# A two-layer sparse-attention encoder: an earlier first block of the gated units, and the copies of transposed probabilities moved from ScalarE to VectorE

## What is computed

```python
proj = h @ w_in                       # q, k, v, index q, index k, index weights, u
score = sum_h relu(iq_h @ ik) * iw_h  # keys are ranked by it, the best are kept
logits = q @ k / 8, others masked;  p = softmax(logits);  attn = p @ v
a, b = split(u);  g = a * sigmoid(b)  # gated units, 512 channels
y = silu(layer_norm(depthwise_conv31(g) + conv_b))
x = x + gate_a * (concat(attn, y) @ w_out)
x = x + gate_f * mixture_of_16_experts(norm(x))
```

## Time and profile before

| | us |
|---|---|
| median of 3 executions | 1450.54 (1449.70 to 1452.48) |
| the profiled execution's own time | 1449.31 |
| its span, first to last instruction | 1447.5 |
| TensorE / VectorE / ScalarE busy | 1253.6 / 569.4 / 368.4 |
| mean granted TensorE clock | 0.914 of full speed |

### The profile page before, as it was taken

The page is one execution under the profiler, slowest core; times in us unless marked ns, Lnnn a source line. Parts: engine busy times, 40 slices in busy tenths (PEclk is TensorE's granted clock), DMA queues, the critical chain, the costliest instruction groups (busy, mean ns, idle before and its releaser), DMA issues.

```text
span 1447.5 us, 16324 instructions
## 1 busy us (share of the span) xinstructions
PE 1253.6 (87%) x6291; PEld 733.4 (51%) x6291; DVE 569.4 (39%) x1478; ACT 368.4 (25%) x861; POOL 152.4 (11%) x218
## 2 busy tenths in 40 slices
PE   4898699987889998999837989899686999999990
PEld 0452254543545586777523533454345457777760
DVE  1227689123236531111107257980323455111115
ACT  2214120035741111111114133001468111111111
POOL 0312050010000150000020113200100011000002
PEclk7899899997999999999967989899858999999995
DMA  9428997260960479999953120224121016799985
GB/s 362 133 69 324 352 341 228 82 228 5 313 230 30 160 211 386 356 369 365 325 184 115 59 71 30 65 67 137 35 56 25 0 68 221 252 365 361 369 289 210
DMA packets 136887, 283.95 MB, mean 196 GB/s; under 512 B 11581, under 2 KB 91877, under 8 KB 130409
## 3 DMA queue, kind: packets, MB, share of 16 engines
q1 hardware_dynamic: 116128, 208.66, 42.7%
q0 software_dynamic: 8352, 42.50, 8.5%
q10 hardware_dynamic: 12329, 31.74, 6.2%
HBM read 236.86 MB, written 52.40 MB: 200 GB/s over the span
## 4 chain that ended last, share of the span: by engine, by line
PE 69%; DVE 11%; DMA 7%; ACT 6%; issue 3%; SPq 2%; ACTq 1%; POOLq 0%; POOL 0%; DVEq 0%
PE ps L508 44%; PE ps L813 9%; PE ps L518 5%; PE ps L671 3%; DMA W<-in_w_gate 3%; PE ps L732 3%; ACT arena L1194 2%; SPq L419 2%; DMA X<-in_x_sample 2%; DVE arena L1498 2%; PE ps L859 2%; DVE small L1497 1%; DVE arena L1537 1%; DVE arena L1588 1%; PE ps L632 1%
## 5 line engine op out<-in xcount | busy, mean ns | idle before, releaser
L508 PE MATMUL ps<-W,arena 128*128 128x256 f32 (+1 forms) x1280 | 348.1, 428 | 10.3 <-DMA W<-in_w_up 5.2
L508 PEld LDWEIGHTS ps<-W,arena 128*128 128x128 f32 x1280 | 242.2, 193 | 85.4 <-issue 49.9
L508 PE MATMUL ps<-W,hT 128*128 128x512 f32 (+3 forms) x480 | 195.0, 563 | 9.7 <-DVE gt L1369 6.6
L518 PE MATMUL ps<-C,arena 128*128 128x128 f32 (+3 forms) x835 | 118.4, 282 | 55.6 <-DVE arena L1417 18.1
L813 PE MATMUL ps<-W,hT 128*128 128x512 f32 (+1 forms) x320 | 144.7, 606 | 5.7 <-ACT hT L1251 5.7
L518 PEld LDWEIGHTS ps<-C,arena 128*128 128x128 f32 (+3 forms) x835 | 95.6, 148 | 96.6 <-issue 36.1
L508 PEld LDWEIGHTS ps<-W,hT 128*128 128x128 f32 (+1 forms) x480 | 87.4, 186 | 110.3 <-issue 83.4
L508 PE MATMUL ps<-hT,W 128*128 128x128 f32 (+1 forms) x512 | 129.4, 414 | 7.1 <-ACT arena L1118 7.1
L508 PEld LDWEIGHTS ps<-hT,W 128*128 128x128 f32 x512 | 79.1, 193 | 58.4 <-issue 50.5
L1805 DVE TENSOR_TENSOR arena<-arena,ps 128x256 f32<-128x256 f32 x32 | 13.5, 421 | 221.7 <-ACT arena L1292 221.7
L813 PEld LDWEIGHTS ps<-W,hT 128*128 128x128 f32 (+1 forms) x320 | 57.1, 183 | 79.9 <-issue 73.6
(11 more groups left out here) (250 smaller groups left out, 1174.1 us busy)
## 6 DMA issues: line engine op xcount, KB each, us to landing
W<-in_w_ada SPq DMA_DIRECT2D x48, 1024.0 KB, 7.4
W<-in_w_gate SPq DMA_DIRECT2D x32, 1024.0 KB, 10.6
W<-in_w_up SPq DMA_DIRECT2D x32, 1024.0 KB, 13.1
W<-in_w_down SPq DMA_DIRECT2D x32, 1024.0 KB, 7.8
y_d<-arena ACTq DMA_DIRECT2D x33, 512.0 KB, 7.3
W<-in_w_in SPq DMA_DIRECT2D x16, 1024.0 KB, 8.5
arena<-x_d SPq DMA_DIRECT2D x31, 512.0 KB, 11.5
arena<-arena SPq DMA_DIRECT2D x128, 79.2 KB, 2.1
```

What stands on the lines that cost most here:

```text
L508: ins = T.matmul(out, l, r, start=n == 0, stop=n == len(pairs) - 1, skip_group_check=True)
L518: count(T.transpose(o, i, ident[0:m, 0:m]), done if n == len(outs_ins) - 1 else None)
```

## The change

Two parts. TensorE's `u_block(0)` no longer waits for all 32 relus at its start: it waits for 30 of them before its first product into `ps[7]`. `u_block(1)` waits for 32 as before. And the copies of the transposed chunks are VectorE's (`copied`, a new function), first in each of its rounds; ScalarE's round becomes `normalised(n + 1)`, `outputs(n - 1)`, `exps(n + 2)`.

```diff
                 def u_block(i):

                     c = 3 + i // 2
-                    pe.wait_ge(*((s_glu, 4 * l + i - 1) if i >= 2 else (L["rel"], 32)))
+                    if i >= 2:
+                        pe.wait_ge(s_glu, 4 * l + i - 1)
+                    if i == 1:
+                        pe.wait_ge(L["rel"], 32)
                     for ab, smp in ((0, 0), (1, 0), (0, 1), (1, 1)):
+                        if i == 0 and smp and ab == 0:
+                            pe.wait_ge(L["rel"], 30)
...
-                for n, (t, g) in enumerate(GROUPS):
-                    m = rows_of(t)
+                for n in range(len(GROUPS)):
+                    if n + 1 < len(GROUPS):
+                        normalised(n + 1)
                     if n >= 1:
                         outputs(n - 1)
-                    for q, (c, kn) in enumerate(chunks_of(t)):
-                        job = PT0[n] + q
-                        act.wait_ge(L["pt"], job + 1)
-                        S.copy(pT[0:kn, c, 0:4 * m], ps[4 + job % 2][0:kn, 0:4 * m]).then_inc(L["pta"], 1)
-                    if n + 1 < len(GROUPS):
-                        normalised(n + 1)
                     if n + 2 < len(GROUPS):
                         exps(n + 2)
...
+                def copied(n):
+
+                    t, g = GROUPS[n]
+                    m = rows_of(t)
+                    for q, (c, kn) in enumerate(chunks_of(t)):
+                        job = PT0[n] + q
+                        dve.wait_ge(L["pt"], job + 1)
+                        V.tensor_copy(pT[0:kn, c, 0:4 * m], ps[4 + job % 2][0:kn, 0:4 * m]).then_inc(L["pta"], 1)
...
                 for n in range(len(GROUPS)):
+                    copied(n)
                     if n + 1 < len(GROUPS):
                         inverses(n + 1)
                     if n + 2 < len(GROUPS):
```

## The result

Forecast 1449.4 us, range 1445.0 to 1455.0. Measured: **1442.63 us**, median of 6 executions (1438.03 to 1446.21), against 1450.13 for the kernel before, 6 executions (1449.64 to 1456.18). The ratio is 0.9939, with a 95% interval of 0.9916 to 0.9963: 5 to 12 us faster, outside the range. The profiled execution took 1442.1 us, its span 1440.2 us (before 1447.5), its mean granted clock 0.916 (0.914).

A forecast was written before the change was run, and what follows sets the result against it. TensorE was taken as the bound, busy 1253.6 of 1447.5 us and 69% of the chain. Terms +2.4 - 11.7 + 7.0 + 1.2 = -1.1 us took the median 1450.5 to 1449.4 us, range 1445.0 to 1455.0.

The forecast's parts named there:

- Both first steps: Layer 1: the 7.13 us idle before `u_block(0)` return as about 8.7 us of DMA wait before `conv(0)`; gain 0.
- What the move buys is order: Attention: with copies on VectorE, transposes and logits run during ScalarE's exponentials; -11.7 us in all.
- -6.9 and -4.8: Attention rounds of layer 1 and layer 0: us gained from TensorE's shorter waits for copies.
- the ends' +3.2 and +3.8: Attention's end, layers 1 and 0: round 9's copies delay VectorE's long reciprocal, costing 3.2 and 3.8 us.
- the output projections' +0.6 twice: Output projection of each layer: longer TensorE idling ahead of it costs 0.6 us of lower clock, +1.2 together.
- The +2.4 for the clock: Layer 1's `conv(0)`: after its new wait it runs at the lower clock, costing 2.4 us, bounds 0 to 2.9.
- that execution is 1.2 us below the median: Whole kernel: the profiled execution, 1449.3 us, lies 1.2 below the median of three, so the forecast starts from 1450.5.
- A shift at either attention passes on in full: After both attentions: experts and their loads start from the attention, so its gain or loss reaches the total undiminished.
- The lower clock ends earlier: Rival, layer 1's attention: denser work brings full clock back some 10 us sooner, 4 us more gain; 1445.4 us, chance 0.14.
- The clock costs nothing more: Rival, `conv(0)` and output projections: the +2.4 and +1.2 fall away; -4.7, or 1445.8 us, chance 0.14.
- The first rounds give nothing: Rival, round 2 of the attentions: waits of 3.16 and 2.9 us only change name; +5.0, or 1455.5 us, chance 0.17.
- the first part does nothing: Rival, layer 1: `u_block(0)` still starts at 910, so the 2.4 are not paid; -3.5, or 1447.0 us, chance 0.08.

The follow-up runs named there:

- e13: Kernel before, with rounds 0 to 4's copies on VectorE, the earlier block, and ScalarE issuing eight of sixteen shifted transfers ahead of both sigmoids: 0.9890, 1432.83 us.
- e12: Kernel before with all copies on VectorE, but behind the next round's reciprocal in place of first: 1.0018, 1452.38 us.
- e2: Kernel before with only the copies moved to VectorE, first in each round, without the earlier block: 0.9942.
- e3: The kernel before again, unchanged, as a measure of the scatter: 0.9989.
- e9: Kernel before with the copies of rounds 0 to 4 on VectorE and the earlier block, one queue: 0.9919, 1438.39 us.

## Why the prediction was wrong

**Right.** Both first steps: in layer 1 the gap moves from ahead of `u_block(0)` to ahead of `conv(0)` (8.7 forecast, 7.71 measured), no gain; and e13 shows that the DMA's issue is what keeps it. "What the move buys is order": e12 shows it by taking the order away. -6.9 and -4.8 were -7.0 and -4.7, the ends' +3.2 and +3.8 were +3.4 and +4.2, the output projections' +0.6 twice were +0.7 and +0.8. For copies under 4 us of waits were forecast, 3.9 came (the second product's 2.0 apart).

**The +2.4 for the clock** was right against the profile it was read from (+2.0; the convolutions' busy time is 33.3 us there and 35.8 in the profile after), but that profile was a cheap one. From the last relu to the attention, layer 1 took 110.86 us in it; over the ten kernels with one queue and the old block it is 111.7 on the mean (110.7 to 113.0), over the four with the earlier block 112.9. So the price against the kernel before is about 1.2: it had often paid the same lower clock already, at another place. The totals of the four pairs that differ by the block (-1.9, -0.4, -2.5, +4.1 by the ratios, mean -0.2) are too wide to confirm or refute that. Half of the term was the profile's luck, since "that execution is 1.2 us below the median" was corrected for in the total, and not in the stage.

**The step that failed** is the last one of the sum: "A shift at either attention passes on in full: what follows it (experts, their loads behind the scatter) starts from it." It starts from it, but does not take as long: the lower clock falls on other matmuls. The sum has no term for that, so it put it at nothing, without a reason. Layer 0's `first_rows` stage is 20.7 us with the old attention and 17.5 with nearly any other, longer or shorter. That is 3.2 us of the 7 to 8, 4.2 up to 594 us, and the only part that follows the kernels, in 17 of 18 profiles. The other 3.4 between the two profiles lie in the experts' stretch (384 to 389 us over all 18 profiles; near 720 us the clock alone makes 3.2 us of difference between profiles of the same code), the start (314.2 to 316.1 with one queue) and the tail, and are as much scatter of one execution as anything; e2, without the earlier block, has 388.0 in the experts' stretch and the same median as the change. What remains open is how the medians' 7.5 us divide, and how much of them the stage makes, since only one execution of each kernel was profiled.

**The rivals.** "The lower clock ends earlier" was the nearest in time (1445.4), but did not happen in layer 1 of the change, where it lasted from 1044 to 1075, 31 us, as before. It is not fixed, though: 41 us in e3, the kernel before again, and 20.5 us in e9 (clock 0.50 from 1042.7 to 1063.2, then 1.00). "The clock costs nothing more" (1445.8) is wrong in its mechanism: the clock did cost at `conv(0)` and both projections, and gave back elsewhere. The Trainium skill (TensorE: Matmul & The Clock Gate, part 1) says of the ramp at a kernel's start that it varies from run to run with the gate's phase there, and is under 1% of a typical kernel span. For one stretch the trace agrees in size: 3.25 us at one stage is 0.2% of the span, and profiles of the same code differ by as much. All of the kernel's lower clock together is more, with a mean of 0.914. For a change worth 0.5% such shares are the size of the error. "The first rounds give nothing" is refuted (0.16 us for 3.16), "the first part does nothing" too (`u_block(0)` starts before the last relu).

The range was too narrow for a reason that the profile could have given: it took in the bounds of my own terms, and nothing for the lower clock elsewhere. A mean granted clock of 0.914 over 1447.5 us means some 250 us at half speed (0.086 x 2 x 1447.5), in stretches that a shift of some us can move to other matmuls. Three us each way for that, the size of the one that did move, would have taken the range down to 1442.

## What to carry to other kernels

When a copy stands between two products of the busiest engine, put it ahead of whatever its engine waits for from a slow neighbour; the engine matters less (692 ns for 586 showed no cost, the place behind the reciprocal cost 9.5 us of the rounds: e12 against e2). Before an earlier start is priced, find the serial resource behind it: here 16 issues at 0.6 us on one queue gave 7 us back, and a second queue took 4 of them. And cut two profiles at the same instructions, stage by stage, before believing a total: terms right to half a microsecond summed to -0.6 while the kernel gained 7.

## What the runs showed that I had not expected

The same 132 matmuls took TensorE 18.92 us or 15.67, by when they came. A pure delay of 3 us in layer 0 was followed by 3.25 us less in the next stage, of which about half came back in the one behind it. And a clock at half speed for some 10 us came into layer 0's attention in 4 of 18 profiles; in e13 TensorE had been busy for 9.65 of the 10 us before it fell (349.3 to 359.3). And more was not better: moving the copies of rounds 0 to 4 alone (1432.9) is no worse than moving those of rounds 0 to 8 (1436.5), and 7 to 10 us better than moving all ten.
